# A hybrid SSD / Conformer / MoE decoder step: order of units, row copies, residual turns, weight issue and the last adds

## The reference

```python
mod = silu(c) @ w_ada + b_ada            # 6 segments: sh1, sc1, g1, sh2, sc2, g2
h = rmsnorm(x) * (1 + sc1) + sh1
z, xbc, dt, glu_in, gate_ssd, gate_conf = split(h @ w_in)
y = grouped_rmsnorm(ssd(conv4(xbc), dt) * silu(z)) @ w_ssd_out
v = silu(layernorm(conv31(glu(glu_in)))) @ w_conf_out
x = x + g1 * ((sigmoid(gate_ssd) * y + sigmoid(gate_conf) * v) @ w_o)
h2 = rmsnorm(x) * (1 + sc2) + sh2
x = x + g2 * moe(h2)                     # 4 groups x 8 experts, best group, its 2 best experts, SwiGLU of width 256
return rmsnorm(x)                        # and the new recurrent and convolution states
```

## Time and profile before

| what | us |
|---|---|
| three runs: median (lowest, highest) | 2112.47 (2112.07, 2113.38) |
| the profiled execution | 2123.28 |
| its span | 2121.5 |
| busy: TensorE, VectorE, GpSimd, ScalarE | 1941.4, 737.4, 273.2, 243.7 |
| mean granted clock of TensorE | 0.959 of 2.4 GHz |
| DMA traffic | 512.58 MB, mean 242 GB/s |

### The profile page before, as it was taken

How to read it: one execution, slowest core, us unless ns; L and a number is a source line. 1 busy time by engine, 2 the same in 40 slices (tenths; PEclk the granted TensorE clock), 3 DMA queues, 4 the chain that set the end, 5 groups by cost and what they waited for, 6 DMA issues and landing times.

```text
span 2121.5 us, 32522 instructions
## 1 busy us (share of the span) xinstructions
PE 1941.4 (92%) x12849; PEld 1422.0 (67%) x12849; DVE 737.4 (35%) x1622; ACT 243.7 (11%) x591; POOL 273.2 (13%) x454
## 2 busy tenths in 40 slices
PE   7599999999989999999999999999988898778874
PEld 3177777776667777777767767766776676556652
DVE  3135756656120133321655541100033222322235
ACT  1010000001140000011222220011120100000002
POOL 1013241505000000000111110010011111111101
PEclk9799999999999999999999999999979989999998
DMA  9965754554675334426544475669348999999994
GB/s 381 386 229 183 281 181 159 185 173 152 225 272 164 119 120 145 131 79 195 154 142 126 144 253 192 217 231 352 131 174 369 411 378 424 418 397 401 400 402 186
DMA packets 243667, 512.58 MB, mean 242 GB/s; under 512 B 18047, under 2 KB 208699, under 8 KB 213683
## 3 DMA queue, kind: packets, MB, share of 16 engines
q1 hardware_dynamic: 232765, 494.75, 63.9%
q0 software_dynamic: 10784, 16.21, 2.2%
HBM read 498.70 MB, written 37.15 MB: 253 GB/s over the span
## 4 chain that ended last, share of the span: by engine, by line
PE 79%; DMA 16%; DVE 2%; issue 1%; ACT 1%; SPq 0%; POOL 0%; DVEq 0%; POOLq 0%; ACTq 0%
PE bank L1312 45%; DMA ring<-in_w_exp_up 7%; PE bank L1547 6%; PE bank L1831 6%; PE bank L1320 6%; PE bank L1331 3%; PE bank L1854 3%; DMA ring<-in_w_ada 3%; DMA work<-in_w_exp_up 2%; DMA ring<-in_w_exp_gate 2%; PE bank L1816 1%; PE bank L1533 1%; PE bank L1562 1%; PE bank L1579 1%; PE bank L1380 1%
## 5 line engine op out<-in xcount | busy, mean ns | idle before, releaser
L1312 PE MATMUL bank<-hT,ring 128*128 128x288 f32 x2304 | 567.7, 409 | 3.1 <-DVE hT L2026 3.1
L1312 PEld LDWEIGHTS bank<-hT,ring 128*128 128x128 f32 x2304 | 440.4, 192 | 132.7 <-issue 11.0
L1312 PE MATMUL bank<-work,ring 128*128 128x288 f32 x1536 | 380.5, 410 | 5.4 <-DMA ring<-in_w_conf_out 4.1
L1312 PEld LDWEIGHTS bank<-work,ring 128*128 128x128 f32 x1536 | 293.2, 192 | 94.2 <-issue 5.6
L1831 PE MATMUL bank<-work 128*64 128x128 f32 x2048 | 133.3, 296 | 38.8 <-issue 29.3
L1831 PEld LDWEIGHTS bank<-work 128*64 128x64 f32 x2048 | 127.8, 151 | 51.2 <-issue 39.3
L1831 PE MATMUL bank<-ring,work 128*64 128x128 f32 x2048 | 127.0, 285 | 38.4 <-DMA ring<-in_w_exp_gate 23.0
L1831 PEld LDWEIGHTS bank<-ring,work 128*64 128x64 f32 x2048 | 120.7, 144 | 51.4 <-issue 36.1
L2087 DVE SCALAR_TENSOR_TENSOR rs<-work,vcol,rs 128x256 f32<-128x256 f32 x232 | 133.7, 576 | 0.0
L1547 PE MATMUL bank<-hT,ring 128*128 128x288 f32 x512 | 131.9, 417 | 0.0
L2087 DVE SCALAR_TENSOR_TENSOR stat<-work,vcol,stat 128x256 f32<-128x256 f32 x232 | 128.4, 553 | 0.0
(11 more groups left out here) (428 smaller groups left out, 1459.7 us busy)
## 6 DMA issues: line engine op xcount, KB each, us to landing
ring<-in_w_in SPq DMA_DIRECT2D x52, 2048.0 KB, 8.1
ring<-in_w_ada SPq DMA_DIRECT2D x48, 2048.0 KB, 12.0
ring<-in_w_exp_down SPq DMA_DIRECT2D x32, 2048.0 KB, 13.8
work<-in_w_exp_gate SPq DMA_DIRECT2D x16, 2048.0 KB, 17.9
work<-in_w_exp_up SPq DMA_DIRECT2D x16, 2048.0 KB, 22.6
ring<-in_w_exp_gate SPq DMA_DIRECT2D x16, 2048.0 KB, 18.0
ring<-in_w_exp_up SPq DMA_DIRECT2D x16, 2048.0 KB, 22.8
ring<-in_w_conf_out SPq DMA_DIRECT2D x8, 2048.0 KB, 9.9
```

Source lines behind the costliest of these rows:

```text
L1312: mm = nc.tensor.matmul(bank[b][:, 0:T], ring[:, s, kk, j * P:(j + 1) * P], rhs[:, kk], start=(kk == 0), stop=(kk == KC - 1))
```

## The change

- Strings of units: "co", "so" and "wo" reordered; the sums of segment 4 in bank 6 instead of 4; in "wo" TensorE waits for the merged input only at the first "p".
- The turn of segment 2 and the tail's turns run behind the first unit of z1.
- rows_in as transposes.
- The nine residual turns run before the first expert, around the gate rows and lists, through banks 6, 7, 1 and 0; only the six spreads stay with the experts, behind 2 to 4. Experts 0 to 4 are written out, the loop has 13 trips.
- SyncE issues each expert weight as its slot comes free; the first expert's gate and up weights go out five units later.
- Tail: TensorE adds the residual of the first prompt block and both addends of the strip into the fold's banks; VectorE scales and joins the strip; the order of the last steps is changed, and ScalarE's tables are asked for ahead of their use.

The diff, without the path for over 64 tokens and without declarations:

```diff
-CO_UNITS = "aaaapppppppp"
-SO_UNITS = "aaaappappappapap"
+CO_UNITS = "aapapapppppp"
+SO_UNITS = "aaaaapapapappppp"
-WO_UNITS = "paapaapaapaapppp"
+WO_UNITS = "apapaapaapaapppp"
...
-        LOOP0, LOOPS = 11, (NE - 12) // 2
+        LOOP0, LOOPS = 5, (NE - 6) // 2
-        X_AT = {2 + n: range(2 * n, min(2 * n + 2, 15)) for n in range(8)}
-        SPREAD0, STRIPS = 9, (9, 14)
+        X_BANKS = [(b, k) for k in range(3) for b in (6, 7, 1, 0)][:9]
+        SPREAD_AT = {2 + n: range(2 * n, 2 * n + 2) for n in range(3)}
+        STRIPS = (0, 5)
...
-            return (4 + seg % 2, 6 + seg % 2) if seg < 2 else (4, 5)
+            return (4 + seg % 2, 6 + seg % 2) if seg < 2 else (6, 5) if seg == 4 else (4, 5)
...
             def first_expert(u):
-                if u == 8:
+                if u == 13:
...
+            def gate_up_weights(e, k):
+                sp.wait_ge(S["g_used"], e - 1)
+                expert_unit(e, 0, k)
+                sp.wait_ge(S["u_used"], e - 1)
+                expert_unit(e, 1, k)
+
+            def down_weights(e, k):
+                sp.wait_ge(S["down_done"], e * 2 - 2)
+                expert_unit(e, 2, k)
+
+            for e in (2, 3):
+                gate_up_weights(e, e - 2)
+            down_weights(2, 0)
-            with sp.Fori(1, NE // 2) as r:
+            with sp.Fori(2, NE // 2) as r:
                 for k in range(2):
-                    for part, (used, per) in enumerate((("g_used", 1), ("u_used", 1), ("down_done", 2))):
-                        sp.wait_ge(S[used], r * (2 * per) + (k - 1) * per)
-                        expert_unit(r * 2 + k, part, k)
+                    gate_up_weights(r * 2 + k, k)
+                    down_weights(r * 2 + (k - 1), 1 - k)
+            down_weights(NE - 1, 1)
...
-            pool.link(gp, gp.tensor_tensor(ya, ya, yb, ALU.add))
-            gp.wait_ge(S["strip_out"], 2)
-            pool.link(gp, gp.tensor_tensor(ya, ya, strip_part, ALU.add))
-            pool.link(gp, gp.tensor_tensor(ya, ya, g2_strip, ALU.mult))
-            gp.tensor_tensor(ya, ya, xstrip, ALU.add).then_inc(S["strip_sum"], 1)
...
+            for n, (q, j) in enumerate(X_ROUNDS):
+                b, k = X_BANKS[n]
+                ac.wait_ge(bank_ready[b], use("xturns", b, k))
+                ac.activation(xstrip if j is None else xrows[:, q, 512 * j:512 * j + 512], bank[b][:], ACT.Copy).then_inc(
+                    bank_free[b], 1)
...
+            ac.activation(ssq[:, 3:4], ones[:, 0:1], ACT.Square)
             for half in range(2):
                 row_squares(0, half)
+            ac.activation(mean_t[:, 3:4], ones[:, 0:1], ACT.Sqrt)
             row_root(1, 0)
-            for h in range(2):
-                ac.activation(strip_part[rows], bank[h][rows], ACT.Copy).then_inc(S["strip_out"], 1)
+            ac.activation(rstd[:, 3:4], ones[:, 0:1], ACT.Square)
             for half in range(2):
                 row_squares(1, half)
...
-            project("glu", hT, rhs_ready=[...])
+            project("glu", hT, rhs_ready=[...], turn_last=False)
             def conv_sums(u):
+                if u == 1:
+                    turn(2)
+                    for j in range(2):
+                        pe.wait_ge(bank_free[j], use("glu", j, 2 * GLU_N - 1))
+                    for q in range(4):
+                        fill("tail", 4 + q)
+                        for n in range(4):
+                            mm = nc.tensor.transpose(bank[4 + q][0:CK - 1 + NS, n * P:(n + 1) * P], utail[:, 4 * q + n], ident[:])
+                        mm.then_inc(bank_ready[4 + q], 1)
...
             project("so", zb, before=group_sums, rhs_ready=[("y_ready", lambda q: q)])
-            pe.wait_ge(S["merged"], KC)
...
+                if n == 0:
+                    pe.wait_ge(S["merged"], KC)
...
                 nc.tensor.matmul(out[:, c % 4], hT[:, c, P * q:P * q + P], ident[:].rearrange("p (i k) -> p i k", i=EG),
-                                 start=(c % 4 == 0), stop=False, skip_group_check=True)
+                                 start=(c % 4 == 0), stop=False, is_transpose=True, skip_group_check=True)
...
             lists("lists", 2, moved, 2 * NE)
+            for n in range(2):
+                x_turn(n)
             for n in range(2):
                 fill("gh", 5, n)
...
+            for n in range(2, 5):
+                x_turn(n)
             pe.wait_ge(S["gates_ready"], 1)
             lists("gates", 4, moved_g, NE)
+            for n in range(5, 9):
+                x_turn(n)
+            for b in (6, 7, 1, 0):
+                pe.wait_ge(bank_free[b], use("xturns", b, sum(x == b for x, _ in X_BANKS) - 1))
...
+                for n in range(4):
+                    fill("fold", FOLD[0][n])
+                    nc.tensor.matmul(bank[FOLD[0][n]][:], ident[:], xrows[:, 0, 512 * n:512 * n + 512], start=True, stop=False)
...
+                pe.wait_ge(y_loaded[2], 128)
+                for w in range(2):
+                    for h in range(2):
+                        nc.tensor.matmul(bank[h][rows], ident[rows, rows], y_in[2][w][rows], start=(w == 0), stop=False)
...
                 expert(NE - 1)
+                fold_in(0)
+                fold_in(1)
                 base_sum(math, 0, 0)
-                fold_in(0)
-                base_sum(math, 0, 1)
-                fold_in(1)
                 base_sum(math, 1, 0)
-                base_sum(math, 1, 1)
...
+            def join_strip():
+                ya = y_in[2][0]
+                for h in range(2):
+                    rows = slice(HD * h, HD * (h + 1))
+                    take("strip_fold", h)
+                    dve.mark(ve.tensor_tensor(ya[rows], g2_strip[rows], bank[h][rows], ALU.mult))
+                dve.wait(ve)
+                ve.tensor_tensor(ya, ya, xstrip, ALU.add).then_inc(S["strip_sum"], 1)
...
             join_half(0, 0)
             join_half(0, 1)
+            base_sum(dve, 1, 1)
+            row_mean(0)
             join_half(1, 0)
-            row_mean(0)
+            row_scale(1, 0)
             join_half(1, 1)
-            row_scale(1, 0)
+            join_strip()
             row_final(0)
+            row_mean(1)
             take("n3", 1)
             ve.tensor_scalar(mean_t[:, 2:3], bank[1][:, 0:1], EPS * D, None, ALU.add).then_inc(S["tail_mean"], 1)
-            row_mean(1)
-            row_scale(2, 2)
+            row_scale(2, 1)
+            row_final(1)
+            row_scale(3, 2)
             ve.scalar_tensor_tensor(out=y_in[2][0], in0=y_in[2][0], scalar=rstd[:, 2:3], in1=fin_strip, op0=ALU.mult,
                                     op1=ALU.mult).then_inc(S["out_rows"], 1)
-            row_scale(3, 1)
-            row_final(1)
```

187 lines of the change are left out of this document (86 added, 101 removed).

## The result

The changed kernel takes 2104.52 us, the median of 13 runs (2096.50 to 2108.40). On the same measurement the kernel before takes 2117.34 (13 runs, 2112.07 to 2128.07). The ratio is 0.9936, 95% interval 0.9923 to 0.9949: 13.6 us faster, between 10.8 and 16.3. Forecast were 23.5 us less and 2089.0, with a range of 2074 to 2102. So the sign was right, the gain was forecast 10 us too large, and the measured time lies 2.5 us above the range. The number misses by 15.5, of which 4.9 come from its base: the median of the three runs shown was 2112.47, that of 13 is 4.9 higher.

A forecast was written before the change was run, and what follows sets the result against it. TensorE's projections bound the kernel to 1537 us, then router steps, expert weight loads, and VectorE, ScalarE and GpSimd in the tail. Terms -3.6 - 13.0 - 6.9 = -23.5 from 2112.5 gave 2089.0 us, range 2074 to 2102.

The forecast's parts named there:

- the six us: Experts 2 to 4: two spreads behind each make them slower than their loads, leaving the weight queue dry some 6 us (2 to 10).
- the -13.0: Experts, first freed slot to first rows of the sum: 493.4 us instead of 506.4, with weights at 0.393 MB/us; ends -21.9, -2.9.
- 13.0 + 6.9: Gains claimed for the experts' weight stream (13.0 us) and for the tail after the first rows land (6.9 us).
- Rival 1: Experts: the weight stream is at its limit, stays at 0.388 MB/us, term -6.9, in all 2095.1 us; chance 0.22.
- rival 2: First experts: TensorE starves the stream; router +7, 15 us lost behind experts 2 to 4, in all 2101 us; chance 0.10.
- forecast 2.6: End of GLU, start of z1: z1's first projection unit covers TensorE's first wait, 2.6 us gained; the second wait stays.
- (3.3): Start of the Conformer projection: first weights loaded in time, unit then limited by ScalarE's input; 3.3 us gained, ends 0 and 5.
- 1.7 were to be gained: Starts of the SSD projection and wo: hidden TensorE waits gain 0.8 us and 0.9 us.
- the sum of 7.6: New unit orders at GLU's end, co, so and wo together: 2.6 + 3.3 + 0.8 + 0.9 us gained.
- Forecast +4: Router: transposed row copies save time, but nine residual turns before the first expert cost more; net 4 us slower, ends 0 and +7.
- forecast 3.6: Everything up to the first expert: projection gains less the router's loss, 3.6 us gained in sum.
- Forecast 28.0 us: Tail, from the landing of the first rows to the end: 28.0 us instead of 34.9, TensorE's added work hidden under VectorE.

The follow-up runs named there:

- sixteenths: Changed kernel with an expert's gathered and scattered rows dealt over the slots in steps of sixteen, not packed from the first: 2089.5 us, 0.9860; same edit in kernel before: 0.9915.
- the second trace: The changed kernel run again with no edit: 2102.37 us, ratio 0.9933 against the kernel before.
- the first two patterns of dealing out: Rows packed from the first slot (changed kernel, 0.9936), and rows dealt in steps of eight in the changed kernel (0.9936) or the kernel before (1.0012).

## Why the prediction was wrong

**Experts: the step that failed.** The step was that "a queue with more in it should at least not do worse" than 0.393 MB/us, and that this rate holds to the last weight. With the six us that the early spreads were to cost, the -13.0 meant -19 for the order by itself; measured are 12.9 (ratio 0.9939). The hole did close, and the queue even moved 0.402 MB/us in the middle, but the forecast took the rate of bytes moved for the rate at which weights arrive. A weight arrives with its slowest DMA engine, which has 4 rows per expert gathered and scattered beside its share of the weights: 14.58 + 4 * 0.32 = 15.9 us, measured 15.9. A deeper queue does not hurry that engine; it lets the others run ahead. By issues the period fell by 0.4 us (16.3 to 15.9), by landings only by 0.14 (16.32 to 16.18, that is 0.389 MB/us), and at the end the others' lead is lost: a mean of 13.2 us over the 16 engines at 2051.5, against 5.0 in the kernel before.

So the 188.7 MB landed in 492.3 us after the first freed slot (1570.28 to 2062.62), where the forecast had 480.2 + 2 + 6 = 488.2. From the first freed slot to the first rows' sum it takes 497.6 us (forecast 493.4, before 506.4): the -13.0 was -8.8. From slot to end the pairs of traces give 13 to 15 us less, where the forecast had 13.0 + 6.9. Rival 1 of the prediction, the stream at its limit, was nearest: its 0.388 and its -6.9 are close to what came, but its reason was not right: 423 GB/s were held, and 419 to the last weight, as soon as the rows were dealt out in sixteenths.

**The limit of one core.** Under the new order the windows without a hole show 419 to 424 GB/s. The Trainium skill, "DMA: Bandwidth & Descriptors", Specifications, has about 358 as the limit of one core; as the forecast said, that is not the limit here.

**Early spreads.** Forecast 6 us lost. The starvation of rival 2 is in the trace (gate issued only at 1649.29, DMA share 0.96 in 1600:1680), but late spreads are worth some 2 us by the medians and 2 to 4 in the traces (slot to end 524.5 against 528.1 and 526.6). The loss comes early and stays: 30 weights have landed 170.0 us after the first freed slot (168.3 in the second trace), against 167.0 with the spreads late, and the last one after 492.3 (491.1) against 489.5. The forecast's 6 was about twice too much, and rival 2's 15 further off.

**Projections.** Over seven executions each, GLU and z1 gained 3.6 us (forecast 2.6) and co 2.6 (3.3). The second wait at GLU's end stayed, and co waits for ScalarE, both as written. At "so" and "wo" the forecast had the sign wrong: from the SSD's last matmul to w_o's last unit it takes 306.4 us and no longer 303.7, 2.8 lost where 1.7 were to be gained. The 3.50 us of the earlier trace rows are gone, but the fifth ada unit and the first projection's weights are waited for instead (1.78 and 4.05 us, shown above), and the slow clock behind adds to it; in the kernel before, the first unit started after 0.28 us and two of them took 31.48 us together:

```profile
1250.66 31.48 PE L1312 MATMUL bank<-work,ring 128*128 128x288 f32 x128 [0.28 <-DVEq L2302]
```

The xbc projection and the SSD, which the change does not touch, came out 1.7 us shorter, within their own scatter of 7.1 us. At the end of w_o that makes 5.1 us; the medians say 3.4 us for all orders (0.9936 against 0.9952), and beside the sixteenths nothing can be told of orders and row copies together; the sum of 7.6 was too much.

**Router.** Forecast +4; +3.0 over the seven (44.4 against 41.4 us from wo's end to the first freed slot). The turns are the smaller part of it: without them it is still 43.1. The traces point to the clock. By their clock records the granted clock left full speed 10.9 to 21.1 us after wo's last unit with the row copies as matmuls (all seven executions); with transposes after 8.1 to 8.8 in ten of eleven, and after 10.8 in the profiled one. So the transposes halve the passes, and the clock falls sooner for all that follows. With the turns late it then stayed at half speed for 34.1 us (all three executions), with the matmuls for 17.1 to 27.3 in all, with transposes and turns for 20.5 to 23.9. The windows of the kernel with turns late show it, columns: length, TensorE busy, clock, DMA, GB/s:

```profile
1535.00:1545.00 10.00, 8.98 (x88) 0.80 0.47 193
1545.00:1555.00 10.00, 10.00 (x38) 0.50 0.39 131
1555.00:1565.00 10.00, 7.34 (x82) 0.50 0.39 138
1565.00:1575.00 10.00, 7.72 (x62) 0.50 0.15 43
```

The Trainium skill, "TensorE: Matmul & The Clock Gate", Part 4, says that transposes do not count as busy; the earlier fall agrees. The turns speak against it: with them the clock was back at 1.00 from 1558.0, between two groups of turns (12 transposes took 2.82 us before and 1.53 after), and so the first expert's gate and up matmuls ran in 7.21 us where they took 10.07 without the turns. That is part of why the turns cost only 1.3 us net.

The prediction set against the rule the 48 transposes from 12 to 26 us with a clock of 1.00. That reading was wrong: the clock record of that trace begins at 29.5 us, and the view prints 1.00 where there is none. The instructions tell it:

```profile
12.35 13.83 PE L1380 MATMUL bank<-ident,work 128*128 128x128 f32 x48 [6.68 <-DMA work<-in_x_sample]
26.11 5.29 PE L1331 MATMUL bank<-ring,work 128*9 128x512 f32 x32
...
32.24 3.62 PE L1331 MATMUL bank<-ring,work 128*9 128x512 f32 x32
```

The same 32 matmuls take 5.29 us and then 3.62; within the first 32 each group of four takes 0.85 us up to 29.5 and 0.43 from there on. So the 48 transposes ran at half speed from first to last (one of 128x128 every 0.26 us, as in the router at 0.50, where eight take 1.97), 13.8 us without a rise, which speaks for the rule. Whether transposes count stays open here.

**Tail.** Forecast 28.0 us from the first rows' sum; measured 30.5, since the second rows' sum waits another 4.66 us for the row loads, which queue behind the last weights. GpSimd is gone from it, TensorE is hidden; -6.9 was -4.4 in the trace, and some 4 by the medians.

**Base.** The differences were carried over one to one onto the median of three runs; 13 runs gave 4.9 us more. And one profiled pair can't carry single terms: up to the first freed slot it shows 9.9 us gained, seven executions of each 2.1 (forecast 3.6).

**The sum.** Of the 15.5 us that the number misses by, the base has 4.9, the experts 4.2, the tail 2.5 and the part up to the first freed slot 1.5; the other 2.4 can't be assigned by single traces. The experts' term or the base alone, put right, would have brought the measured time just into the range.

## What to carry to other kernels

When a weight stream is bound by its DMA engines, look at the 16 landings of one transfer before deepening its queue: if they lie far apart, some engines carry more than others (here gathered and scattered rows in the first slots of a table), and levelling their load, one statement here, gained more than the new order of issues did (0.9915 against 0.9939 in the kernel before). A queue's end must be looked at as closely as its start, since what runs ahead in the middle stands idle at the end. Sum terms of a few us over several executions, not from one pair.

## What the runs showed of the hardware

A weight's 16 landings can lie 20 us apart, and the lead builds up slowly: 3 us at 1611, 8 at 1761, 16 at 1874, 19 to 22 from 1912 on. That a row queue with 5.1% of the engines' time sets the pace of a weight stream at 95.7% was not expected. Slots reach the engines in blocks of four (argued from the first two patterns of dealing out and borne out by the third; which engine carries which block was not seen, the trace names no engine). The same instructions up to the first freed slot took between 1567.9 and 1578.9 us; most of that scatter lies between the start of the xbc projection and the SSD's end (497.5 to 504.6 us), and its cause is open.
